# Expert weights issued by two engines: chunks 0, 2 and 4 by SyncE, chunks 1, 3 and 5 by GpSimd

## What is computed

```python
logits = (x @ p['w_router'] + p['b_router']).astype(jnp.float32)
top_v, top_e = lax.top_k(logits, TOP_K)          # 4 of 32 experts
gate = jax.nn.softmax(top_v, axis=-1)
...
def _expert(xb, e, w_gu, b_gu, w_dn, b_dn):
    gu = xb @ w_gu[e] + b_gu[e]                  # 1024 x 2048
    g = jnp.minimum(gu[..., :D_EXPERT], SWIGLU_LIMIT)
    u = jnp.clip(gu[..., D_EXPERT:], -SWIGLU_LIMIT, SWIGLU_LIMIT)
    act = g * jax.nn.sigmoid(SWIGLU_ALPHA * g) * (u + 1.0)
    return act @ w_dn[e] + b_dn[e]               # 1024 x 1024
```

## Time and profile before

| | |
|---|---|
| Median of 3 runs | 1462.0 us (1460.63 to 1462.52) |
| The profiled execution's own time | 1462.08 us |
| Its span, first to last instruction | 1460.3 us |
| Mean granted TensorE clock | 0.987 of full speed |
| PE busy | 1376.6 us, 94% of the span |
| DVE / ACT / POOL busy | 631.8 / 323.6 / 83.6 us |
| HBM read, written | 495.71 MB, 9.15 MB |

### The profile page before, as it was taken

One profiled execution on the slowest core, in us unless ns is written; L12 is line 12 of the kernel. 1 busy time (PEld: TensorE's weight loads), 2 busy tenths in 40 slices (PEclk: granted clock), 3 DMA queues, 4 the chain that ended last, 5 costly groups with the idle time before them and its releaser, 6 DMA issues.

```text
span 1460.3 us, 21891 instructions
## 1 busy us (share of the span) xinstructions
PE 1376.6 (94%) x8444; PEld 656.8 (45%) x8444; DVE 631.8 (43%) x1574; ACT 323.6 (22%) x598; POOL 83.6 (6%) x126
## 2 busy tenths in 40 slices
PE   4999999999999999999999999999999999999997
PEld 2457777777776533333333333333333333333332
DVE  1274344478773755344234223432333233323333
ACT  3013222266550241111111111111111111111111
POOL 2201000222202100000000000000000000000000
PEclk8999899999999989999999999999999999999999
DMA  9976833444516969999999999999999999999995
GB/s 338 291 266 232 330 136 103 155 168 146 187 75 221 347 261 427 427 428 426 429 427 429 428 427 429 426 429 427 429 427 428 428 427 429 426 429 428 428 428 229
DMA packets 65572, 502.00 MB, mean 344 GB/s; under 512 B 6465, under 2 KB 12533, under 8 KB 40680
## 3 DMA queue, kind: packets, MB, share of 16 engines
q1 hardware_dynamic: 55056, 463.07, 76.7%
q0 software_dynamic: 10464, 38.23, 7.6%
HBM read 495.71 MB, written 9.15 MB: 346 GB/s over the span
## 4 chain that ended last, share of the span: by engine, by line
DMA 45%; PE 44%; DVE 5%; ACT 3%; issue 2%; POOL 1%; SPq 0%; DVEq 0%; ACTq 0%; POOLq 0%
DMA arena<-in_w_gu 42%; PE bank_v L1216 28%; PE bank_s L1216 13%; PE bank_s L1220 2%; DVE arena L1715 2%; ACT arena L2210 2%; DMA arena<-mod_rows 1%; DMA arena<-in_page_table 1%; DVE arena L1727 1%; POOL arena L2434 1%; DMA arena<-in_w_ada 1%; DMA x_rows<-in_x_sample 1%; DVE x_rows L1715 0%; DVE arena L1712 0%; ACT L2210 0%
## 5 line engine op out<-in xcount | busy, mean ns | idle before, releaser
L1216 PE MATMUL bank_v<-arena 128*64 128x512 f32 (+14 forms) x4916 | 817.5, 467 | 45.3 <-DMA arena<-in_w_gu 29.0
L1216 PEld LDWEIGHTS bank_v<-arena 128*64 128x64 f32 (+7 forms) x4916 | 335.5, 137 | 510.3 <-issue 367.0
L1216 PE MATMUL bank_s<-arena 128*64 128x512 f32 (+2 forms) x2004 | 425.6, 505 | 9.0 <-ACT arena L1113 6.6
L1216 PEld LDWEIGHTS bank_s<-arena 128*64 128x64 f32 (+2 forms) x2004 | 181.7, 143 | 198.8 <-issue 142.9
L991 DVE TENSOR_SCALAR arena<-bank_v 128x512 f32<-128x512 f32 x32 | 22.1, 692 | 413.7 <-PE bank_v L1216 413.7
L1013 DVE TENSOR_TENSOR arena<-bank_v,arena 128x512 f32<-128x512 f32 x128 | 82.5, 686 | 122.7 <-PE bank_v L1216 122.7
L1110 ACT ACTIVATE arena<-arena 128x512 f32<-128x512 f32 x32 | 20.2, 630 | 387.8 <-DVE arena L991 387.8
L1220 PE MATMUL bank_s<-const_tables,arena 128*128 128x128 f32 (+3 forms) x605 | 92.8, 284 | 2.0 <-DVE arena L1724 1.1
L1220 PEld LDWEIGHTS bank_s<-const_tables,arena 128*128 128x128 f32 (+3 forms) x605 | 71.0, 169 | 50.1 <-issue 32.8
L1018 DVE TENSOR_TENSOR x_rows<-x_rows,arena 128x512 f32<-128x512 f32 x128 | 82.8, 688 | 2.2
L1715 DVE TENSOR_TENSOR arena<-bank_v,arena 32x128 f32<-32x128 f32 (+10 forms) x124 | 46.7, 377 | 66.6 <-PE bank_v L1216 39.7
(11 more groups left out here) (124 smaller groups left out, 638.9 us busy)
## 6 DMA issues: line engine op xcount, KB each, us to landing
arena<-in_w_gu SPq DMA_DIRECT2D x128, 2048.0 KB, 24.1
arena<-in_w_dn SPq DMA_DIRECT2D x64, 2048.0 KB, 21.6
arena<-in_w_ada SPq DMA_DIRECT2D x12, 2048.0 KB, 12.1
arena<-in_w_in SPq DMA_DIRECT2D x10, 2048.0 KB, 12.8
arena<-in_state_win_kv POOLq DMA_DIRECT2D x8, 512.0 KB, 7.0
arena<-in_w_out SPq DMA_DIRECT2D x2, 2048.0 KB, 19.5
out_win_sample<-in_state_win_kv POOLq DMA_DIRECT2D x1, 4064.0 KB, 28.0
x_rows<-in_x_prompt POOLq DMA_DIRECT2D x4, 512.0 KB, 8.8
```

Of the source, the lines that this page charges most:

```text
L1216: return pe.matmul(out, l, r, start=first, stop=last)
```

## The change

SP keeps chunks 0, 2 and 4, and POOL takes 1, 3 and 5, for the first expert and for all reloads. The waits of each chunk stay what they were, but each engine now has only its own. POOL's loads of the first expert stand among its small loads: chunk 1 behind the router's loads and ahead of the nine moves of the bias, chunks 5 and 3 between these and the loads of `gate2`. Its loop of reloads stands behind the loads of `gate2` and ahead of the addition at the end.

```diff
+        def reload(queue, chunks_of, e1, expert):
+            for k in chunks_of:
+                if k < 4:
+                    queue.wait_ge(sem("gu_filled"), 4 * e1 - 3 + k)
+                else:
+                    queue.wait_ge(sem("dn_filled"), 2 * e1 + (k - 5))
+                load_chunk(queue, k, expert)
+
+        def reloads(queue, chunks_of):
+            with queue.Fori(1, NEXP) as e:
+                reload(queue, chunks_of, e, e)
+            queue.wait_ge(sem("over_known"), 1)
+            n = queue.value_load(over_n[0:1, 0:1], min_val=0, max_val=OVER)
+            with queue.If(n > 0):
...
         def pool_late(pool, dma):
...
             dma(brt, bc(A["b_router"][0], P), "router_loaded")
+            ring, m = chunk_last[("up_a", 0)]
+            pool.wait_ge(sem(f"{ring}_filled"), m)
+            load_chunk(pool, 1, 0)
             pool.wait_ge(sem("bias_parts"), 1)
...
+            pool.wait_ge(sem("bias_placed"), 16 * 9)
+            load_chunk(pool, 5, 0)
+            ring, m = chunk_last[("out", 1)]
+            pool.wait_ge(sem(f"{ring}_filled"), m)
+            load_chunk(pool, 3, 0)
             pool.wait_ge(sem("v_filled"), tags["v"].index(("router", 1)) + 1)
...
+            reloads(pool, (1, 3, 5))
             pool.wait_ge(sem("first_rows"), 1)
...
         def sp_late(sp):
             sp.wait_ge(sem("v_filled"), tags["v"].index(("up_a", 3)) + 1)
-            load_chunk(0, 0)
-            load_chunk(2, 0)
-            ring, m = chunk_last[("up_a", 0)]
+            load_chunk(sp, 0, 0)
+            load_chunk(sp, 2, 0)
+            ring, m = chunk_last[("out", 1)]
             sp.wait_ge(sem(f"{ring}_filled"), m)
-            load_chunk(1, 0)
-            sp.wait_ge(sem("bias_placed"), 16 * 9)
-            load_chunk(5, 0)
-            for k in range(3, 5):
...
+            load_chunk(sp, 4, 0)
+
+            reloads(sp, (0, 2, 4))
```

More of the change, by code:

```diff
@@ L1123, in se_late, with load_chunk @@
             barrier(se, "se")
+        def load_chunk(queue, k, e):
+            wg, wd = A["w_gu"][0], A["w_dn"][0]
+            if k < 4:
+                src = wg[bass.ds(e, 1), k * 256:(k + 1) * 256, :]
+            else:
+                src = wd[bass.ds(e, 1), (k - 4) * 512:(k - 3) * 512, :]
+            queue.dma_start(eslots[k], src.rearrange("o (p t) n -> p (o t n)", p=P)).then_inc(sem(f"expert_weights_{k}"), 16)
+        def reload(queue, chunks_of, e1, expert):
+            for k in chunks_of:
+                if k < 4:
+                    queue.wait_ge(sem("gu_filled"), 4 * e1 - 3 + k)
+                else:
+                    queue.wait_ge(sem("dn_filled"), 2 * e1 + (k - 5))
[6 more added lines that the diff above has]
+            with queue.If(n > 0):
+                with queue.Fori(0, n) as b:
+                    expert = queue.value_load(over_e[0:1, bass.ds(b, 1)], min_val=0, max_val=NEXP - 1)
+                    reload(queue, chunks_of, NEXP + b, expert)
         def pool_late(pool, dma):
```

## The result

The changed kernel took 1473.05 us in the median of 4 runs (1471.01 to 1474.42), the kernel before 1461.63 (4 runs, 1460.63 to 1462.52). The ratio is 1.0074 (95% interval 1.0059 to 1.0089): slower by 0.74%, some 11 us. The profiled execution took 1471.01 us with a span of 1469.4, 9.1 us longer than the span of before, 1460.3. Those 9.1 us are what the two traces can explain; the median lies 2 us higher than this execution.

The account below looks back on a forecast made before the run. One DMA byte stream up to the last expert's chunk 3, then a fixed tail, was taken to bound the kernel. Issuing 0, first fill 0, order +1.5, packets 0 on 1462.08 gave 1463.6 us; range 1455 to 1473.

Parts of the forecast that it names:

- the price of a packet: Loop with two queues: alternating 16 KiB packets cost nothing more, 0 us; bounds +4.6 and -6.2 us over the stream.
- a late POOL: Loop: POOL starts loads late, d at its bound 9.81, ending at 1467; slower packets or later chunk 3 together 0.37.
- dearer packets or a later chunk 3: Rival, DMA-bound loop: alternating costs 3.1 ns a packet, 1468.2 us, or chunk 3 lands later; chance 0.37.
- What bounds the kernel: Expert loop from 732 us: one DMA byte stream at 428 GB/s, 29.42 us a block, PE waiting at chunk 3.
- the addition stays free: 0: POOL's end: 96 added loads, 48 us, fit its idle time, so its final 1.27 us addition costs nothing.
- fixed tail of 28.7 us: From the last expert's chunk 3 at 1433.37 to the end at 1462.08, taken as unchanged.
- the term of +1.5: Loop's chunk order: chunk 3 lands d - 4.90 later, 0.8 us reckoned, 1.5 taken for POOL's start; bounds 0 and 4.9.
- The lag d: Distance of chunk 3's landing behind chunk 2's in the loop: 4.90 us with one queue, 5.7 with two.
- Sharing: Engines alternate packet by packet between both queues: half the bandwidth each, 9.81 us a chunk, stream no longer.
- 4.2 ns cheaper packet: Rival, loop's packets: alternating hides time on each packet, 6.2 us less, 1457.4 us; chance 0.20.
- First fill: Before the loop: chunk 1 delays w_out's second half 4.9 us to 481.4, covered by 0.6: 0 us, bounds 0 and 1.4.
- Do nothing: Rival, loop order: d stays at 4.90, so 1462.1 us; chance 0.43 together with the forecast.

## Where the prediction was right and where it was wrong

The forecast was 1463.6 us, within 0.2% of before; the kernel is 0.74% slower, at 1473.05, at the very top of the range (1455 to 1473). That the range reaches so far is luck: its width came from the price of a packet and a late POOL, and neither happened. The slower side was in the rivals, as dearer packets or a later chunk 3; chunk 3 did come later, but at the lag of the forecast itself, and the larger part of the loss, the drain, stood in none of them.

**What bounds the kernel.** Right. 428 GB/s, 29.4 us a block and one wait a block at chunk 3 stand in the profile after as they were forecast.

**The part that failed: "the addition stays free: 0", and with it the fixed tail of 28.7 us.** From chunk 3 to the end of the span it is 1460.3 - 1433.37 = 26.9 us before and 1469.4 - 1437.24 = 32.2 after. The addition is free. But the part asked only what POOL computes at the end, and the tail holds the barrier, where POOL's drain answers for every load issued since the last one. Ninety-six loads more made it 7.2 us longer (11.03 - 3.84); 5.2 of them came behind everything else, since the old 3.84 us had slack. This is the larger of the two misses, and a term that the sum did not have. The trace of before showed a drain of 3.84 us on an engine with little to do, and I didn't ask what it was made of.

**Order: the term of +1.5 was mis-sized; 4.1 was measured, 2.9 of it order.** Chunk 3's matmuls were to start at 1434.9 and start at 1437.24. The lag d was right, the formula was not. "SP's chunks keep their place in the average stream, so chunk 3 lands d - 4.90 later" forgets that chunk 3 runs beside chunk 2 for 9.81 - d and delays it too. It is simpler to count what goes ahead of chunk 3 that didn't before: in its last d us half the bandwidth goes to chunk 4, which is d / 2. By the prediction's own d = 5.7 that is 2.85 us.

The traces bear this out. Each of the 16 engines reports its part of a chunk by itself, and the trace keeps these times, though no view prints them. Of the last expert, the mean of the 16 times for chunks 2, 3 and 5, and the last of the 16 for chunk 3:

| Kernel | Chunk 2, mean | Chunk 3, mean | Chunk 5, mean | Chunk 3, last engine |
|---|---|---|---|---|
| before | 1426.66 | 1431.57 | 1441.36 | 1433.33 |
| changed | 1429.23 | 1434.97 | 1441.90 | 1437.19 |
| POOL drained early | 1430.62 | 1436.36 | 1443.29 | 1438.54 |

Chunk 3 lies 5.74 behind chunk 2 in both kernels with two queues, which is the d of the prediction. Reckoned from the first reload, chunk 5, where the stream ends, is 0.76 late in the changed kernel, and chunk 3 on the mean 3.62: 2.86 for order, half of 5.74. The last engine, for which PE has to wait, is 2.22 behind the mean where it was 1.76, which is 0.46 more; why was not tested. 2.86 + 0.76 + 0.46 is the 4.09 of the table but for rounding. The run with the early drain gives 2.86, 0.67 and 0.42 in the same way, and the runs whose last chunks came by one queue, or with chunk 1 alone on POOL's, no order within 0.1.

The 0.76 is a thinner start: POOL's first reload goes out at 530.49, and from 530 to 538 us the engines move less than in the same window of before, shown first:

```profile
530.00:538.00 8.00, 8.00 (x46) 2.73 (x44) 6.31 (x7) 4.62 (x5) 0.00 (x0) 1.00 1.00 430
```

```profile
530.00:538.00 8.00, 8.00 (x48) 2.84 (x44) 6.16 (x8) 4.36 (x5) 1.10 (x2) 1.00 0.98 393
```

That is 8 x (430 - 393) / 428 = 0.7 us of stream that never comes back. The run with chunks 4 and 5 on POOL's queue has hardly a thin start (0.25) and more order (5.4 on the mean of the engines, with 2.0 for the last one), because both of its chunks are needed after chunk 3: +7.65 in all.

**Sharing.** Right in kind. From 473 to 476 us, where 16 KiB packets of chunk 1 meet the small ones of `w_out`, the counts are even:

```profile
q0 software_dynamic: 68, 1.07, 84.5%
q1 hardware_dynamic: 67, 0.14, 12.3%
```

The Trainium skill's rule in "DMA: Bandwidth & Descriptors", section "Queues, rings and completion order", that an engine drains typically 9 to 17 descriptors from one ring before it turns, was weighed as a sum of 0. With whole chunks alternating, chunk 3 would not be 2.9 us late by order, so the measurement stands against it here. So do the packets' own times. From 800 to 1400 us of the changed kernel every packet starts within 4 ns of the end of another, which puts them in 16 rows, one for each engine, and in these all 17,611 neighbours are of different queues.

**Price of a packet: 0.** Right; 428 GB/s with one queue, with two and, in the run with all reloads by POOL, with the software queue alone. So neither the 3.1 ns dearer nor the 4.2 ns cheaper packet exists with 16 KiB on both sides, and both packet rivals fall. The Trainium skill's page "DMA: Bandwidth & Descriptors", section "Issuing engines are not separate DMA queues", says that DMAs of several engines run on the same 16 DMA engines and that issuing from more of them saves only issuing time; the trace agrees, and issuing time was not on the path.

**First fill.** Right: the second half of `w_out`, the longer of the two loads of this line, landed 31.0 us after its issue at 449.8, at 480.8 (forecast: 481.4):

```profile
DMA to landing us min/median/max: 12.6/21.8/31.0
```

PE did not wait for it, and the loop began 0.22 us earlier. The run with all loads by POOL showed that the cover can go: 4.3 us at that wait, and a loop 8.7 us late.

**Do nothing, or a late POOL.** The idle case needed d = 4.90; by the corrected count even that would cost 4.90 / 2 = 2.5 us. A POOL that is late by more and more was not seen: the lag is 5.74 in the 11th block and in the last.

## What to carry to other kernels

This stream of DMAs, in the order of use and already filling the engines, had nothing to gain from a second issuing queue, and lost what the second queue carried ahead of the transfer that is waited for. In such a case count that: the bytes needed later that get ahead of the last chunk on the path. When work of any kind moves to an engine, look also at what that engine does at the end of a stage or of the program, its drain above all, and if it grows, drain it early beside other work.

## What the runs showed of the hardware

- GpSimd's drain grew by 82 ns for each DMA issued since its last drain, whether it moved 16 KB or 2 MiB and though it had landed: 3.84 us after 30, 11.26 after 123, and only 2.27 after 154. With nothing issued since, 1.39 us, 1.27 of them the addition.
- Two queues with packets of 16 KiB took turns packet by packet on every engine: 17,611 of 17,611 neighbours from 800 to 1400 us, at 428 GB/s as with one queue.
- The start of the loop differs between runs. Kernels with the same program up to there sent the first reload at 526.24 to 528.00 us. TensorE's granted clock is at half (1.2 GHz of 2.4) from 510 to 516 us and rises at another moment from run to run; from 516 to 520 us, first in the kernel before, then with chunk 1 by POOL, where PE stood within 0.1 us until 514.2 and the loop began 2.4 us later:

```profile
516.00:520.00 4.00, 4.00 (x20) 1.71 (x16) 0.19 (x1) 0.60 (x1) 0.00 (x0) 0.84 0.01 2
```

```profile
516.00:520.00 4.00, 4.00 (x12) 0.78 (x8) 0.00 (x0) 0.17 (x1) 0.00 (x0) 0.50 0.00 1
```

That is the part of the spread between runs which the distance in the table leaves out. Whether a kernel's own change moves that moment was not tested.
